# Weights of the dense layers: one load and one split per half of 2048 columns, two raw slots in place of four of 1024

## The reference, cut to what matters

```python
def swiglu(h, w_in, w_out):
    gate, up = jnp.split(h @ w_in, 2, axis=-1)
    return (jax.nn.silu(gate) * up) @ w_out

for l in range(DEPTH_2):                                  # 2 layers
    x = x + 0.5 * swiglu(rms_norm(x, ffa_norm[l]), ffa_w_in[l], ffa_w_out[l])
    h = rms_norm(x, mix_norm[l])
    (c_q, c_kv, k_rope, g_q, g_k, g_v, g_b, g_a, g_z, m_qkv, gate_logits) = split_cols(h @ w_in[l], IN_SPLITS)
    ...                                                   # three branches: mla, gdn, moba
    gates = jax.nn.sigmoid(gate_logits.reshape(b, s, N_BRANCH, D_MODEL))
    x = x + jnp.sum(gates * up, axis=2) @ w_out[l]
    x = x + 0.5 * swiglu(rms_norm(x, ffb_norm[l]), ffb_w_in[l], ffb_w_out[l])
```

## Time and profile before

| | us |
|---|---|
| median of 3 runs | 2466.55 |
| lowest and highest | 2465.05, 2469.44 |
| the profiled execution: its own time | 2466.87 |
| its span, first to last instruction | 2465.0 |
| TensorE busy in the span | 2426.4 (98%) |
| GpSimd busy | 1010.1 (41%), all of it after 1056 us |
| ScalarE, VectorE busy | 887.1, 924.0 |

### The profile page before, as it was taken

One profiled execution on the slowest core, in us unless ns is written; L12 is line 12 of the kernel. 1 busy time (PEld: TensorE's weight loads), 2 busy tenths in 40 slices (PEclk: granted clock), 3 DMA queues, 4 the chain that ended last, 5 costly groups with the idle time before them and its releaser, 6 DMA issues.

```text
span 2465.0 us, 34958 instructions
## 1 busy us (share of the span) xinstructions
PE 2426.4 (98%) x13879; PEld 1715.0 (70%) x13879; DVE 924.0 (37%) x1746; ACT 887.1 (36%) x1455; POOL 1010.1 (41%) x428
## 2 busy tenths in 40 slices
PE   8999999999999999999999999999999999999999
PEld 6744444444444444468889899888888898998887
DVE  5622222222222222253238764332432378653322
ACT  6411111111111111154457634544444477425443
POOL 0000000000000000038878445788788795546986
PEclk9999999999999999999999999999999999999999
DMA  7799999999999999935555333465555553324554
GB/s 285 292 399 428 430 430 429 430 429 430 430 429 430 429 430 430 381 120 199 189 168 178 105 103 129 155 209 189 177 189 193 169 175 120 120 95 154 200 185 144
DMA packets 96703, 653.66 MB, mean 265 GB/s; under 512 B 10880, under 2 KB 13232, under 8 KB 69968
## 3 DMA queue, kind: packets, MB, share of 16 engines
q1 hardware_dynamic: 96592, 652.11, 68.1%
HBM read 651.01 MB, written 1.06 MB: 265 GB/s over the span
## 4 chain that ended last, share of the span: by engine, by line
PE 87%; DMA 9%; DVE 1%; ACT 1%; issue 1%; POOL 0%; SPq 0%; DVEq 0%; ACTq 0%
PE bank L2221 20%; PE bank L831 13%; PE bank L631 10%; PE bank L633 10%; PE bank L632 10%; PE bank L832 7%; DMA ring<-in_expert_units 5%; DMA scratch<-in_expert_units 4%; PE bank L2208 4%; PE bank L1226 3%; PE bank L2229 2%; PE bank L2551 1%; PE bank L2237 1%; PE bank L1104 1%; PE bank L1075 1%
## 5 line engine op out<-in xcount | busy, mean ns | idle before, releaser
L618 POOL TENSOR_TENSOR w_lo<-raw,w_hi 128x1024 fp32r<-128x1024 f32 (+2 forms) x424 | 1009.9, 2410 | 1442.5 <-ACT w_hi L612 1442.5
L2221 PE MATMUL bank<-ring,scratch 128*64 128x512 f32 x2304 | 514.1, 596 | 12.8 <-DMA ring<-in_expert_units 11.7
L831 PE MATMUL bank<-hT_both,w_hi 128*128 128x512 f32 x1408 | 496.2, 398 | 1.7 <-DVE hT_both L722 1.7
L612 ACT CAST w_hi<-raw 128x1024 fp32r<-128x1024 f32 (+2 forms) x424 | 421.1, 1042 | 166.6 <-PE bank L633 159.2
L832 PE MATMUL bank<-hT_both,w_lo 128*128 128x256 f32 x1408 | 394.8, 280 | 0.0
L2221 PEld LDWEIGHTS bank<-ring,scratch 128*64 128x64 f32 x2304 | 160.5, 137 | 327.6 <-issue 321.7
L831 PEld LDWEIGHTS bank<-hT_both,w_hi 128*128 128x128 f32 x1408 | 264.7, 188 | 67.0 <-issue 3.0
L2461 DVE TENSOR_TENSOR scratch<-bank,scratch 128x512 f32<-128x512 f32 x64 | 44.3, 692 | 597.3 <-PE bank L2237 593.2
L832 PEld LDWEIGHTS bank<-hT_both,w_lo 128*128 128x128 f32 x1408 | 265.9, 189 | 0.6
L909 DVE TENSOR_REDUCE scratch<-bank 128x256 f32<-128x512 f32 x88 | 60.9, 692 | 356.6 <-PE bank L832 356.6
L2221 PE MATMUL bank<-scratch 128*64 128x512 f32 x768 | 172.1, 596 | 3.1 <-DMA scratch<-in_expert_units 3.1
(11 more groups left out here) (380 smaller groups left out, 3371.9 us busy)
## 6 DMA issues: line engine op xcount, KB each, us to landing
ring<-in_expert_units SPq DMA_DIRECT2D x144, 2048.0 KB, 29.6
raw<-in_layer_halves SPq DMA_DIRECT2D x408, 512.0 KB, 3.9
scratch<-in_expert_units SPq DMA_DIRECT2D x48, 2048.0 KB, 30.5
ring<-in_first_units SPq DMA_DIRECT2D x11, 1024.0 KB, 10.4
scratch<-in_ple_units SPq DMA_DIRECT2D x2, 2048.0 KB, 11.0
raw<-in_layer_halves SPq DMA_DIRECT2D x8, 424.0 KB, 3.2
scratch<-in_norm_gains SPq DMA_DIRECT2D x6, 512.0 KB, 5.8
raw<-in_layer_halves SPq DMA_DIRECT2D x4, 384.0 KB, 3.2
```

Of the source, the lines that this page charges most:

```text
L612: k.nc.scalar.copy(k.w[0][i % SPLIT_SLOTS][:, at], k.raw[n % RAW_SLOTS][:, 0:at.stop - at.start]).then_inc(k.shared("weights_hi"), 1)
L618: k.nc.gpsimd.tensor_tensor(k.w[1][i % SPLIT_SLOTS][:, at], k.raw[n % RAW_SLOTS][:, 0:at.stop - at.start], k.w[0][i % SPLIT_SLOTS][:, at], ...
L831: nc.tensor.matmul(bank[:, :], w[0], both, start=start, stop=False)
L2221: last = nc.tensor.matmul(b[g * SL:(g + 1) * SL, :], lhsT[:, c, :], w[:, c, g, :], start=start and c == 0, stop=stop and c == 3)
```

## The change

A half is one piece. It is loaded by one transfer of up to 2048 columns, rounded by one cast and subtracted by one GpSimd instruction. Two raw slots of 2048 columns stand in place of four of 1024, in the same memory. The load of half n waits until half n - 2 has been split. The counts that TensorE waits for are halved accordingly. In the first part of the program, which uses the same four landing semaphores for other loads, nothing changes but a constant's name.

```diff
-RAW_SLOTS, SPLIT_SLOTS = 4, 3
+RAW_SLOTS, SPLIT_SLOTS, FIRST_RAW = 2, 3, 4
...
-        self.raw = [sb(f"raw{i}", [P, HALF // 2]) for i in range(RAW_SLOTS)]
+        self.raw = [sb(f"raw{i}", [P, HALF]) for i in range(RAW_SLOTS)]
...
 def pieces(i):
 
-    words = words_of(HALVES[i % len(HALVES)]) // 2
-    return [(2 * i + j, slice(j * words, (j + 1) * words)) for j in range(2)]
+    return [(i, slice(0, words_of(HALVES[i % len(HALVES)])))]
...
     for n, at in pieces(i):
-        act.wait_ge(k.later_arrived[n % RAW_SLOTS], 16 * (n // RAW_SLOTS + 1 + 2 * FIRST_UNITS // RAW_SLOTS))
+        act.wait_ge(k.later_arrived[n % RAW_SLOTS], 16 * (n // RAW_SLOTS + 1 + 2 * FIRST_UNITS // FIRST_RAW))
...
-    pe.wait_ge(k.shared("weights_split"), 2 * i + 2)
+    pe.wait_ge(k.shared("weights_split"), i + 1)
...
-    pe.wait_ge(k.shared("weights_split"), 4)
+    pe.wait_ge(k.shared("weights_split"), 2)
```

More of the change, by code:

```diff
@@ L131, in __init__ @@
         self.stored = sem("output_stored")
-        self.later_arrived = [sem(f"later_weights_arrived{i}") for i in range(RAW_SLOTS)]
+        self.later_arrived = [sem(f"later_weights_arrived{i}") for i in range(FIRST_RAW)]
         self.bank_full = [sem(f"bank_full{b}") for b in range(8)]
@@ L479, in first_hi_act @@
         elif n == 2 or half and c % 4 == 0:
-            act.wait_ge(k.later_arrived[half % RAW_SLOTS], 16 * (half // RAW_SLOTS + 1))
+            act.wait_ge(k.later_arrived[half % FIRST_RAW], 16 * (half // FIRST_RAW + 1))
         scale = k.f("g_mix")[:, c:c + 1] if unit < 4 else 1.0
@@ L1786, in load @@
             sp.dma_start(k.ring[half // 2 % 2][:, at:until], dram["first_units"][half // 2, :, at:until])\
-                .then_inc(k.later_arrived[half % RAW_SLOTS], 16)
+                .then_inc(k.later_arrived[half % FIRST_RAW], 16)
         load(0)
```

## The result

| | before | after |
|---|---|---|
| median of 4 runs, us | 2467.06 | 2555.53 |
| lowest and highest, us | 2465.05, 2469.44 | 2548.12, 2558.12 |
| ratio, with 95% interval | | 1.0347, 1.0326 to 1.0368 |
| span of the profiled execution, us | 2465.0 | 2552.6 |
| its mean granted TensorE clock | 0.999 | 0.991 |

The kernel became 88 us slower, 3.5%. The forecast was 2493, 26 us slower, with a range up to 2530: the sign was right, the ffn blocks and the mixing parts were rightly named as the places, and the size was not.

What follows compares the result with a forecast made beforehand. TensorE, busy 2426.4 of 2465.0 us, was taken as the bound. Feed-forward loop 12.0, places without slack 10.4 and ScalarE's delayed work 4 made 26.4 over 2466.87: 2493 us, range 2472 to 2530.

Steps and rivals of the forecast that it cites:

- The three new durations: Per half of 2048 columns: subtraction about 4.6 us, cast 1.90 us, landing of the 1 MB load 4.75 us.
- 3.3 us of slack: Steady feed-forward stretch: a half is split 3.3 us before TensorE begins it; 2.7 would go at once, 0.6 remain.
- the loop of landing, cast and subtraction through two raw slots: Feed-forward blocks: 11.37 us for two halves, 5.69 a half against TensorE's 5.585, so 0.10 us a half lost.
- short transfer: Rival: landing below 4.5 us, loop shorter than TensorE's pace, only places without slack paid; 2474 to 2478 us; chance 0.14.
- not slower: Rival: fewer, often shorter GpSimd instructions and landing by 4.4 us keep places without slack on time; 2463 to 2471; chance 0.13.
- Part 3: Feed-forward blocks: loop through two raw slots costs 2.7 us twice in ffn0 and 3.3 twice in ffn1, sum 12.0.
- The rival of the long transfer: 1 MB lands in 5.05 us, loop 5.84 a half, 2517 us; at 5.45, 2545 us; chance 0.23.
- Part 4: Places without slack at ffn1's start and in mixing parts: 5.2 us a layer, 10.4; ScalarE's delayed other work, 4.
- the 1.0 of the last half: Last half before ffn1, in Part 4: 1.0 us for a load that leaves later.
- its 0.7: Last half before ffn1, in Part 4: 0.7 us, since each split is done that much later.

Runs made afterwards that it cites:

- The experiments with four slots: Changed kernel with each half landing in its low part's slot, no raw slots, a fourth split slot: 2574.05 us; the same with casts one half later: 2502.8 us.
- the kernel with three slots: The kernel before with three raw slots of 1024 columns in place of four, nothing else: 2498.68 us, median of three runs.
- the first wait was filled: Four split slots in place with later casts, plus 20 unread matmuls ahead of TensorE's longest wait in each layer's mixing part: 2493.77 us.

## Why the prediction was wrong in size

**Right.** The three new durations; that TensorE had 3.3 us of slack and that it would be used up; that the loop of landing, cast and subtraction through two raw slots takes over in the ffn blocks, with casts waiting for the landing and not for a bank; the direction. The rivals "short transfer" and "not slower" fell: in no block was the mean round below 11.17.

On the subtraction the Trainium skill, "GPSIMD Engine Reference", Elementwise — side-by-side cycle accounting, gives 4497 ns for a `tensor_tensor` add of 2048 float32 columns. The trace has 4641 as the mean of the 204 subtractions of that width, which agrees within 3.2%.

**The step that failed most is Part 3's sum, 12.0 us; it measured 44.** The base round is as predicted: two loads of 4.7 to 4.8 us give 11.39 to 11.5 (start of the cast 0.08, not 0.02). But I put the median landing into a loop whose time follows the mean. In the blocks the mean is 5.07, since about every fifth load needs some 6 us. Both kinds in the view of transfers, one load each:

```profile
raw<-in_layer_halves SPq DMA_DIRECT2D x1, 1024.0 KB, 4.7
...
raw<-in_layer_halves SPq DMA_DIRECT2D x1, 1024.0 KB, 6.0
```

They left at 1200.94 and 1207.65, through the same queue. With 5.07, 0.08 and 0.15 us of waiting for GpSimd, a half takes 11.84 / 2 = 5.92 and the drift is 0.33 us a half, not 0.10. Times 33 halves and four blocks that is 44. The rival of the long transfer named this landing, 5.05, and gave 2517. Its number for the landing was right, and whether its reason was is open. The prediction held against it that the loads mostly run alone; in the trace 117 of the 206 loads behind the first six overlap another. The 24 that left when another had over 0.3 us still to go landed in 4.87 on average, the others in 4.95. The 59 during which another was issued took 5.12, the others 4.87, but a late load has more time to be joined by the next, so this need not be an effect of overlap.

**The second is a term that was left out: the norms behind the blocks, 12.5 us.** I wrote that ScalarE's other work in the ffn blocks costs nothing when held up, which is true of the silu. But behind the last casts of a block stands the norm's square. ScalarE and then VectorE at the end of ffn0:

```profile
1282.27 1.62 ACT L611 CAST w_hi<-raw 128x1696 fp32r<-128x1696 f32 x1 [3.29 <-DMA raw<-in_layer_halves]
1283.91 1.28 ACT L764 ACT_TABLE_LOAD   x1
...
1285.31 0.61 ACT L683 ACTIVATE h_rows<-x_res 128x512 f32<-128x512 f32 x1
```

```profile
1280.13 0.69 DVE L935 SCALAR_TENSOR_TENSOR x_res<-bank,x_res 128x512 f32<-128x512 f32 x1 [10.18 <-PE bank L632]
...
1286.66 0.15 DVE L703 TENSOR_SCALAR scratch<-scratch 128x1 f32<-128x1 f32 x1 [3.12 <-ACT h_rows L683]
```

The first half row to square is there at 1280.8; ScalarE stands in front of a landing until 1282.27, squares at 1285.31, and TensorE idles. The experiments with four slots show this term by itself: 23.1 us of such waits with the casts early, 1.9 with them late.

**The third is Part 4, 10.4 + 4 = 14.4 us; the mixing parts measured 30.** Its own working has two slips of little weight: 1338.1 - 1335.77 is 2.3 and not 2.5, and the terms of a layer make 5.2 only if the 1.0 of the last half holds its 0.7. The one place I worked out was near: `gdn,0,1` was to make TensorE wait 2.5 us, and it waits 3.90. Its low part took 7.0 us against the 6.9 of Part 4; the row holds this subtraction and the next, and answers to the earlier trace rows. GpSimd and TensorE:

```profile
1350.17 11.56 POOL L617 TENSOR_TENSOR w_lo<-raw,w_hi 128x2048 fp32r<-128x2048 f32 x2 [3.54 <-ACT w_hi L611]
```

```profile
1357.27 0.58 PE L630 MATMUL bank<-hT_both,w_hi 128*128 128x256 f32 x1 [3.90 <-POOL w_lo L617]
```

What I did not price is what such a wait does to the clock. Windows of the changed kernel, behind this wait and around the norm of 1289:

```profile
1345.00:1365.00 20.00, 16.10 (x82) 14.32 (x82) 19.37 (x24) 9.64 (x12) 13.20 (x3) 0.83 0.48 166
```

```profile
1270.00:1290.00 20.00, 15.12 (x67) 12.01 (x66) 5.07 (x9) 8.67 (x12) 15.17 (x4) 0.94 0.48 158
1290.00:1300.00 10.00, 10.00 (x48) 9.39 (x47) 4.79 (x11) 5.42 (x12) 0.97 (x1) 0.78 0.20 83
```

Each is a wait of 4 us or so with 6.8 us at half clock, of which 1.5 us still fall in the wait; the other 5.3 cost some 2.7 us more. All seven stretches cost some 15 us, spread over the mixing parts and what follows the norms, and the prediction had 0. Five of the seven go with waits of 3.7 to 5.2 us. The other two, near 1407 and 2141, follow the two waits of 2.6 us of L630 for "issue" in the rows above, for which the profile names nobody. The kernel before has these two waits as well, at 1.5 us and with no half clock behind them:

```profile
PE bank L631 <- issue: 3.0, 2, 1.5
```

Why they grew is open.

**What the runs say of the cause.** Cutting cast and subtraction in two gives back 68 of 88 us with the slots as they are; taking the raw-slot round away gives back 53 (2555.5 to 2502.8) with both whole, but only with the casts moved one half later as well: without that the kernel was 18 slower. With all of it done 6 remain, which the interval does not part from none. That the round binds in the blocks rests on the distances of the splits, 5.88 to 5.92 us with the change and 5.49 to 5.57 with half the bytes. So there are two causes and they overlap: a round longer than TensorE's, and splits that are done 0.7 us and more later at the places without slack. The rows let both act on TensorE partly through ScalarE, which stands in front of a landing with other work behind it; with four slots this is shown by the 71 us, with two slots it is only read from the rows, since moving one cast gained nothing. Not tried: a kernel whose casts stand on an engine with nothing else to do. The 12 us of the mixing parts that the pieces do not explain are not shown to come from the raw slots: the kernel without them and with later casts lost 35 there.

## What to carry to other kernels

Before two stations are merged or a buffer is taken away, write down the whole round of a slot (reissue, mean landing, each operation) against what the consumer takes for as many units, and keep the margin large: with a third to spare, as before, next to nothing waited; with 2%, in the kernel with three slots, some 30 us were lost. Take the landing from the kernel that is to be built, if it can be had: with fewer slots it was longer both times, 5.07 where 4.75 and 4.55 where 3.9 had been put in. The first page of the Trainium skill, "Trainium Kernel Development and Optimization", Best Practices, asks to double-buffer so that transfer and compute overlap; here, in the dense blocks, two buffers did not do it when the round took 11.84 us against 11.17 for two units of the consumer, and did when half the bytes made it shorter. Then look at which in-order engine waits for the landing and what stands behind that wait: in the kernel with four slots moving it by one unit was worth 71 us, with no size changed. And count a wait of TensorE of 4 us as 4 plus the half clock that goes with it, here another 2.7.

## What the runs showed of the hardware that I had not expected

**Late landings go with instruction packets.** I set each of the changed kernel's 206 loads behind the first six beside the packets of kind "instruction" in the same trace. With none in flight between 1.5 us after its issue and its landing, a load lands in 4.74 us on average, and none of 150 is over 5.5. With one of 16 KB (48 loads) the average is 5.58, and 28 of the 29 loads over 5.5 are of these; the last has one of 8 KB. The queues in the window of the load of 6.0 us (packets, MB, share of 16 engines), and behind the dots in that of the load of 4.7:

```profile
q1 hardware_dynamic: 152, 1.11, 53.2%
q8 instruction: 1, 0.02, 1.6%
...
q1 hardware_dynamic: 144, 1.05, 61.2%
```

That packet took 1.52 us, the load 1.3 longer. Of the 48 the 20 during which another load was issued took 5.91 (17 of them late) and the 28 others 5.34 (11 late); of the 150 the same two groups took 4.71 and 4.75. In the kernel with four slots and later casts, where loads seldom overlap, only 4 of 37 loads with such a packet were late. So the packet is not enough by itself, and no run takes it away: a strong coincidence, not a shown cause.

**Two transfers land later than one.** A pair of 512 KB issued together landed 5.40 us after the first issue, one of 1 MB 4.94, half of that amount alone 3.82.

**One stretch at half clock more went than was aimed at.** In layer 0 of the profiled execution a later wait of 4.2 us (for VectorE's L1655) and the 6.8 us at half clock behind it went as well when the first wait was filled; in layer 1 both stayed. Why is open.
